# Splitting the state readout of an S5 block into quarters between quarters of a gate unit

## The chip, the cores and the metric

The kernel runs on one NeuronCore of a Trainium2 chip. Its engines are TensorE (PE, matmuls), VectorE (DVE), ScalarE (ACT), GpSimd (POOL) and SyncE (SP); the last two mostly issue transfers here, which all run on the core's 16 DMA engines. The metric is the device time of one execution in microseconds (us), as the median of several runs.

## The reference

One transformer-like block on 256 tokens of width 1024, in float32. The parts around the change:

```python
def s5_readout(h_re, h_im, c_re, c_im):
    y = (jnp.einsum('blgn,ghn->blgh', h_re, c_re) - jnp.einsum('blgn,ghn->blgh', h_im, c_im))
    return y.reshape(y.shape[0], y.shape[1], S5_WIDTH)
...
y_a, y_ac = s5_mixer(u_a, u_ac, ...)          # two scans (forward, backward), readout, then s5_glu
y_b = sgu_mixer(z_b, ...)
...
def s5_glu(y, w, b):
    y = jax.nn.gelu(y)
    return y * jax.nn.sigmoid(y @ w + b)

def merge_branches(y_a, y_b, gate_logits, w_proj_a, w_proj_b, b_gate, w_out):
    g_a, g_b = jnp.split(jax.nn.sigmoid(gate_logits + b_gate), N_BRANCH, axis=-1)
    return (g_a * (y_a @ w_proj_a) + g_b * (y_b @ w_proj_b)) @ w_out
```

Behind it come a modulated norm and a convolutional feed-forward part (`w_up`, a 3 x 3 depthwise convolution, `w_down`). The modulation vectors are `c_silu @ w_ada + b_ada`. `gate_logits` are 2048 columns of `h @ w_in`.

## The kernel before

The program of each engine is written out by hand, in its order; semaphores tie them together. An engine does nothing out of order, so a wait holds up all that stands behind it.

The scan works in chunks of eight tokens. The output of a token is a part from within its chunk (a Toeplitz product, L638) plus what the states carried into the chunk give, the **carry readout** (L651). Both add up in PSUM banks 0 and 1: bank `g2` takes groups of parity `g2`. The readout loops over the two banks, the directions `d` and real and imaginary parts `r`, and 16 groups: 128 matmuls of 64 rows by 32 columns of weights on 128 columns, written as one block of 64 for bank 0 and one of 64 for bank 1. It waits for `s_scan`, VectorE's last carry.

**Gate units** (`gate_unit`, L556) are the eight products that give `gate_logits`, 16 matmuls of 128 x 128 on 256 columns each. Their weights come through a ring of four slots (`ring_w`). Units 1 to 5 run ahead of the Toeplitz product, unit 6 between it and the readout, unit 7 behind the readout. After them PE transposes the eight pieces of the scan's output (L661), does three half projections with y_b (L670), the GLU product (L688), the half projection of m = 3, and then the second halves and the later projections, m = 0 to 7; then the products with w_out (L711, `out_product`).

What the others do there:

- ScalarE copies banks 0 and 1 to SBUF (L921) once `s_y8_ps` is 2, does the sigmoids of gate unit 7 (L880), the gelu (L929), and the sigmoids of the GLU (L933).
- VectorE does `modulation_sums` (L1402): 28 dot products, each on a tile of `mod_w` (512 KB) in one of seven slots. Sums 0 to 11 and L1407 stand ahead of the y rows (L1415, scan output plus skip), sums 12 to 17 behind them, then the four y_a products (L1423), sums 18 and 19, and then the merges of m = 0 to 7 (L1434 to L1437) with one sum, 20 + m, behind each of the first six. L1444 and L1448 prepare the products of L711.
- POOL's queue (q0) loads the tiles of `mod_w`, tile t once sum t - 7 is done. Between tiles 19 and 20 stands the **ga1 store** (L379), 1024 single float32 elements written to a scratch tensor in HBM; ahead of it POOL waits for `s_y8_ps` 2 and `s_ga1`.
- SP's queue (q1) loads ring units: unit u once unit u - 4 has been multiplied. Unit 19 (needed by m = 4 and 5) follows gate unit 7, and after it come a wait for `s_y8_ps` 2 and `out_w[0]`; unit 20 (m = 6 and 7) and `out_w[1]` follow the GLU product.

Of the kernel before, what the change touches and what calls it, by code (L numbers as in the profile page):

```python
# [22 lines left out]
P = 128  # L23
D = 1024
KD = D // P
TOK = 256
# [8 lines left out]
T = 8  # L35
# [9 lines left out]
RING = 4  # L45
# [3 lines left out]
U_ADA1, U_INU, U_V, U_ZU, U_GATE = 0, 2, 4, 6, 8  # L49
GATES = 8  # L50
# [30 lines left out]
def build(nc, x_t, x_tok, ctx_t, pk, s5raw, early_w, ring_w, out_w, up_w, ln, sgu_w, sgu_b, mod_w, c_row, g_row, out):  # L81
    with ExitStack() as ctx:
# [6 lines left out]
        bank = [ctx.enter_context(nc.psum_tensor(f"bank{i}", [P, 512], F32)) for i in range(8)]  # L89
# [6 lines left out]
        ca = ca_region.rearrange("p (d r q e h) -> p d r q e h", d=2, r=2, q=PAIRS, e=T + 1)  # L96
# [24 lines left out]
        h_x = h_all[:, :, TOK:2 * TOK]  # L121
# [7 lines left out]
        ring = ring_region[:, :].rearrange("p (s n) -> p s n", s=RING)  # L129
# [85 lines left out]
        s_unit = sem("unit_multiplied")  # L215
# [25 lines left out]
        s_e_ps, s_e, s_ev, s_scan = sem("e_in_psum"), sem("e_evacuated_by_act"), sem("e_evacuated_by_dve"), sem("carry_ready")  # L241
        s_gate = sem("gate_ready")
        s_mod2, s_scale2 = sem("mod2_ready"), sem("scale2_ready")
        s_y8_ps, s_y8, s_y_tr = sem("y_by_chunk_in_psum"), sem("y_by_chunk_ready"), sem("y_transposed")
# [36 lines left out]
        def ring_ready(pe, u):  # L281

            pe.wait_ge(s_ring[u % RING], 16 * (u // RING + 1))
# [116 lines left out]
        def _(pe):  # L400
# [21 lines left out]
            for k in range(KD):  # L422
                pe.wait_ge(s_sqx[k % 2], k // 2 + 1)
                mx = partial_squares(bank[6], k, TOK)
            mx.then_inc(s_part, 1)
            for k in (1, 2, 0, 3, 5, 6, 4, 7):
                by = next(e for e in range(3) if k in CTX_SQUARES[e])
                pe.wait_ge(s_sqc[by], CTX_SQUARES[by].index(k) + 1)
                mx = partial_squares(bank[7], k, 0)
# [87 lines left out]
            for half in range(2):  # L517
                u = U_V + half
                ring_ready(pe, u)
                for c in range(2):  # L520
                    for kk in range(KD // 2):
                        k = half * (KD // 2) + kk
                        mx = pe.matmul(bank[6 + c][:, :], h_x[:, k, c * P:(c + 1) * P], ring[:, u % RING, kk * 512:(kk + 1) * 512],  # L523
                                       start=(k == 0), stop=(k == KD - 1))
# [8 lines left out]
            for i in range(2):  # L533
                u = U_ZU + i
                ring_ready(pe, u)
                for mm in range(2):
                    for k in range(KD):
                        mx = pe.matmul(bank[2 + i][:, mm * TOK:(mm + 1) * TOK], ring[:, u % RING, (mm * KD + k) * P:(mm * KD + k + 1) * P],
                                       h_x[:, k, :], start=(k == 0), stop=(k == KD - 1))
# [16 lines left out]
            def gate_unit(j):  # L556
                u = U_GATE + j
                ring_ready(pe, u)
                if j >= 2:
                    pe.wait_ge(s_gate, 2 * (j - 1))  # L560
                for mm in range(2):
                    for k in range(KD):
                        mx = pe.matmul(bank[5 - j % 2][:, mm * TOK:(mm + 1) * TOK], ring[:, u % RING, (mm * KD + k) * P:(mm * KD + k + 1) * P],  # L563
                                       h_x[:, k, :], start=(k == 0), stop=(k == KD - 1))
                mx.then_inc(s_unit, 1)
# [15 lines left out]
            for m in range(KS):  # L581
                base = (m % 2) * LAGS * H
                for d, r, e0, j0 in ((1, 0, 1, 0), (1, 1, 1, 0), (0, 0, 0, T - 1), (0, 1, 0, T - 1)):
                    for q in range(4 * m, 4 * m + 4):
                        row = 32 * (q % 4)
                        mx = pe.matmul(bank[6 + m // 2][row:row + 32, base + j0 * H:base + (j0 + T) * H],
                                       b_pad[:, r, d * PAIRS + q].rearrange("p g h -> p (g h)"),
                                       ca[:, d, r, q, e0:e0 + T, :].rearrange("p e h -> p (e h)"),
                                       start=(d == 1 and r == 0), stop=(d == 0 and r == 1), skip_group_check=True)
# [11 lines left out]
            for j in range(4):  # L601
                for c in range(2):
                    for g2 in range(2):
                        mx = pe.matmul(bank[6 + j // 2][g2 * 64:(g2 + 1) * 64, (j % 2) * TOK + c * P:(j % 2) * TOK + (c + 1) * P],
                                       v_tok[:, c, (2 * j + g2) * 64:(2 * j + g2 + 1) * 64], sgu_w_sb[:, j, g2 * P:(g2 + 1) * P],
                                       start=True, stop=True)
# [26 lines left out]
            for g2 in range(2):  # L633
                for j in range(P // H // 2):
                    for m in range(KS):
                        g = m * (P // H) + 2 * j + g2

                        mx = pe.matmul(bank[g2][m * CH:(m + 1) * CH, j * P:(j + 1) * P], u_chunk[:, g, CH:2 * CH], m_toep[:, g, :],  # L638
                                  start=(j == 0), stop=False, skip_group_check=True)
# [1 line left out]

            gate_unit(6)

            pe.wait_ge(s_scan, 1)
            for g2 in range(2):
                half = slice(g2 * N, (g2 + 1) * N)
                for d, r, e0 in ((0, 0, 1), (0, 1, 1), (1, 0, 0), (1, 1, 0)):
                    for j in range(P // H // 2):
                        for m in range(KS):
                            q = m * (P // H // 2) + j  # L650
                            mx = pe.matmul(bank[g2][m * CH:(m + 1) * CH, j * P:(j + 1) * P], carry[half, (r * 2 + d) * PAIRS + q, :],  # L651
                                           ca[half, d, r, q, e0:e0 + T, :].rearrange("p e h -> p (e h)"),
                                           start=False, stop=(d == 1 and r == 1), skip_group_check=True)
                mx.then_inc(s_y8_ps, 1)

            gate_unit(7)


            pe.wait_ge(s_y8, 2)
# [137 lines left out]
        def _(act):  # L797
# [118 lines left out]
            gate_sigmoids(6)  # L916


            act.wait_ge(s_y8_ps, 2)
            for b in range(2):  # L920
                act.activation(y_tok.rearrange("p (t g b h) -> p b g t h", t=T, b=2, h=H)[:, b],  # L921
                               bank[b][:, :].rearrange("p (g t h) -> p g t h", g=4, t=T), ACT.Copy).then_inc(s_y8, 1)

# [825 lines left out]
```

## Time and profile before

| | |
|---|---|
| median of 3 runs | 479.42 us (478.02 to 479.83) |
| span of the profiled execution, first to last instruction | 471.4 us |
| PE busy | 454.4 us, 96% |
| DVE busy | 403.4 us, 86% |
| ACT, POOL busy | 105.2 us, 47.3 us |
| HBM traffic | 206 GB/s over the span |

The profiled execution has no total of its own beside its span; what lies around the span is taken from the median, 8.0 us. Times in the rows are counted from the start of the span. A float32 matmul of the program stands as two records. A bracket at the end of a timeline row says how long the engine stood idle before it and what released it. "issue" means that nothing in the profile explains the idle time.

### The profile page before, as it was taken

The numbers are of one execution on the slowest core, as the hardware profiler recorded it, in microseconds if no ns is written. First come the engines' busy times: TensorE is split into PE (matmuls) and PEld (weight loads), VectorE is DVE, ScalarE is ACT, GpSimd is POOL, SyncE is SP. The second block draws the span as 40 slices with busy tenths as digits, with TensorE's granted clock in tenths as the row PEclk, the third lists the DMA queues.
The fourth block names the chain that finished last, engine by engine and source line by source line (L and its number), as shares of the span: only waits on it lengthen the run. The fifth ranks groups of instructions, "written<-read, shape, count | busy, mean of one in ns | idle before, by whom it ended". The sixth has DMA issues, their size and how long they took to land.

```text
span 471.4 us, 7799 instructions
## 1 busy us (share of the span) xinstructions
PE 454.4 (96%) x2670; PEld 350.5 (74%) x2670; DVE 403.4 (86%) x836; ACT 105.2 (22%) x197; POOL 47.3 (10%) x78
## 2 busy tenths in 40 slices
PE   8899999999999899998999999999999999999994
PEld 5677757888888788883578888887888887444454
DVE  4698999999999857869855999998999999899644
ACT  5432344144113014101151211011011011200002
POOL 2001200004030323200000110110111011000000
PEclk9999999999999979999989999999999999999998
DMA  8993489825999999996985443442443444100002
GB/s 302 421 418 139 163 311 98 332 99 94 115 319 413 417 407 334 240 423 246 426 359 222 179 156 118 173 179 95 172 176 108 161 178 135 43 0 1 0 1 89
DMA packets 22107, 97.41 MB, mean 207 GB/s; under 512 B 6528, under 2 KB 7168, under 8 KB 13376
## 3 DMA queue, kind: packets, MB, share of 16 engines
q1 hardware_dynamic: 15024, 74.70, 44.4%
q0 software_dynamic: 5664, 20.72, 14.9%
q10 hardware_dynamic: 1392, 1.63, 1.0%
q8 instruction: 18, 0.29, 0.3%
q14 instruction: 9, 0.07, 0.1%
HBM read 94.44 MB, written 2.59 MB: 206 GB/s over the span
## 4 chain that ended last, share of the span: by engine, by line
PE 69%; DVE 18%; DMA 8%; issue 2%; ACT 1%; SPq 1%; DVEq 0%; ACTq 0%
PE bank L759 31%; PE bank L770 14%; PE bank L563 11%; DVE s_region L1033 8%; DMA s_region<-early_w 4%; DMA s_region<-mod_w 4%; PE bank L711 4%; PE bank L478 3%; PE bank L651 2%; PE bank L688 1%; DVE s_region L1152 1%; PE bank L670 1%; DVE s_region L1290 1%; PE bank L443 1%; DVE merge_tmp L1033 1%
## 5 line engine op out<-in xcount | busy, mean ns | idle before, releaser
L759 PE MATMUL bank<-h_all,s_region 128*128 128x256 f32 x704 | 153.5, 381 | 0.7 <-ACT ctx_region L982 0.7
L759 PEld LDWEIGHTS bank<-h_all,s_region 128*128 128x128 f32 x704 | 134.5, 191 | 19.5 <-ACT ctx_region L982 1.1
L1561 DVE SCALAR_TENSOR_TENSOR ctx_region<-ctx_region,pk_sb 128x189 f32<-128x189 f32 (+2 forms) x352 | 127.6, 437 | 0.2 <-DVE ctx_region L1561 0.2
L563 PE MATMUL bank<-h_all,ring_region 128*128 128x256 f32 x256 | 58.4, 390 | 0.7 <-DVE s_region L1321 0.7
L563 PEld LDWEIGHTS bank<-h_all,ring_region 128*128 128x128 f32 x256 | 49.9, 196 | 8.7 <-DVE s_region L1321 1.0
L770 PE MATMUL bank<-s_region,ring_region 128*128 128x512 f32 (+1 forms) x132 | 47.6, 521 | 0.0
L770 PEld LDWEIGHTS bank<-s_region,ring_region 128*128 128x128 f32 x132 | 25.1, 190 | 22.6 <-issue 21.5
L982 ACT ACTIVATE ctx_region<-bank 128x512 f32<-128x512 f32 x22 | 13.1, 597 | 127.3 <-PE bank L759 70.6
L1402 DVE SCALAR_TENSOR_TENSOR s_region<-s_region 128x1024 f32<-128x1024 f32 x28 | 33.3, 1223 | 7.8 <-DMA s_region<-mod_w 7.5
L1033 DVE TENSOR_TENSOR s_region<-s_region,power 128x2048 f32<-128x2048 f32 (+1 forms) x16 | 38.1, 2420 | 0.2
L395 POOL TENSOR_TENSOR ring_region<-gates,ctx_region 128x256 f32 x22 | 17.2, 784 | 184.6 <-ACT gates L987 184.6
L1551 DVE TENSOR_SCALAR ctx_region<-ctx_region,pk_sb 128x256 f32<-128x256 f32 x44 | 21.0, 521 | 14.5 <-ACT ctx_region L982 13.2
L478 PE MATMUL bank<-h_all,ring_region 128*128 128x256 f32 x128 | 31.2, 389 | 0.0
L670 PE MATMUL bank<-z_region,ring_region 128*128 128x256 f32 x128 | 28.0, 379 | 0.0
L478 PEld LDWEIGHTS bank<-h_all,ring_region 128*128 128x128 f32 x128 | 23.2, 190 | 5.5 <-issue 2.5
L670 PEld LDWEIGHTS bank<-z_region,ring_region 128*128 128x128 f32 x128 | 24.2, 190 | 3.3
L382 POOL DMA_DIRECT2D s_region<-mod_w x28 | 14.8, 538 | 43.1 <-DVE s_region L1402 43.1
L880 ACT ACTIVATE gates<-bank,pk_sb 128x256 f32<-128x256 f32 x16 | 6.7, 470 | 44.2 <-PE bank L563 44.2
L523 PE MATMUL bank<-ring_region,h_all 128*128 128x512 f32 x32 | 16.4, 593 | 0.0
L1002 ACT ACTIVATE z_region<-s_region 128x512 f32<-128x512 f32 (+1 forms) x5 | 2.7, 541 | 52.8 <-DVE s_region L1614 30.0
L511 PEld LDWEIGHTS bank<-ident,s_region 128*128 128x128 f32 x64 | 7.9, 141 | 8.8 <-issue 7.9
L711 PE MATMUL bank<-s_region,h_all 128*128 128x512 f32 (+1 forms) x40 | 14.2, 507 | 0.0
(236 smaller groups left out, 502.6 us busy)
## 6 DMA issues: line engine op xcount, KB each, us to landing
s_region<-up_w SPq DMA_DIRECT2D x33, 1024.0 KB, 4.8
ring_region<-ring_w SPq DMA_DIRECT2D x22, 1024.0 KB, 10.6
s_region<-mod_w POOLq DMA_DIRECT2D x28, 512.0 KB, 10.3
s_region<-early_w SPq DMA_DIRECT2D x4, 1024.0 KB, 21.7
s_region<-out_w SPq DMA_DIRECT2D x4, 1024.0 KB, 11.9
gates<-early_w SPq DMA_DIRECT2D x2, 1024.0 KB, 10.7
s_region<-k_scratch POOLq DMA_DIRECT2D x8, 256.0 KB, 11.8
x_region<-x_t SPq DMA_DIRECT2D x1, 1024.0 KB, 4.9
```

What stands on the lines that cost most here:

```text
L395: pool.tensor_tensor(ffn_act[:, bass.ds(i * 2 + b, 1), :].rearrange("p a t -> p (a t)"), silu_sb[:, b, :], conv[:, b, TOK:2 * TOK], ALU.mu ...
L478: mx = pe.matmul(bank[m][:, cols], ring[:, U_INU + k // 4, ((k % 4) * KS + m) * P:((k % 4) * KS + m + 1) * P], h_all[:, k, cols], start=(k ...
L523: mx = pe.matmul(bank[6 + c][:, :], h_x[:, k, c * P:(c + 1) * P], ring[:, u % RING, kk * 512:(kk + 1) * 512], start=(k == 0), stop=(k == K ...
L563: mx = pe.matmul(bank[5 - j % 2][:, mm * TOK:(mm + 1) * TOK], ring[:, u % RING, (mm * KD + k) * P:(mm * KD + k + 1) * P], h_x[:, k, :], st ...
L670: mx = pe.matmul(bank[PROJ_BANK[m % 4]][:, (1 - half) * TOK:(2 - half) * TOK], ring[:, u % RING, t * P:(t + 1) * P], src[:, k, :], start=( ...
L711: mx = pe.matmul(bank[OUT_BANK[n]][:, cols], lhs(i), rhs(i)[:, cols], start=(i == 0 and n not in (2, 3)), stop=(i == KD // 2 - 1), skip_gr ...
L759: mx = pe.matmul(bank[s % 3][:, half * TOK:(half + 1) * TOK], up_ring[:, s, (half * KD + k) * P:(half * KD + k + 1) * P], h2[:, k, :], sta ...
L770: mx = pe.matmul(bank[PRODUCT_BANK[n]][:, cols], lhs(i), rhs(i)[:, cols], start=(i == 0), stop=(i == PAIRS_D - 1))
L1033: mark(dve.tensor_tensor(o, a, b, op))
L1402: dve.scalar_tensor_tensor(out=mod_tile[t % MTS], in0=mod_tile[t % MTS], scalar=1.0, in1=c_bc, op0=ALU.mult, op1=ALU.mult, accum_out=mod_s ...
L1551: dve.tensor_scalar(dst[half], src[half], cw[:, tile[half], 4], par("conv_b")[:, tile[half]], ALU.mult, ALU.add).then_inc(s_conv, 1)
L1561: dve.scalar_tensor_tensor(out=o, in0=a, scalar=cw[:, tile[half], (dy + 1) * 3 + dx + 1], in1=o, op0=ALU.mult, op1=ALU.add).then_inc(s_con ...
```

## The change

The readout is cut into four quarters, by bank and direction. Gate unit 7 is cut into quarters of four matmuls, by half of its columns and half of its inner dimension, and one follows each quarter of the readout. The waits of the gate unit stand ahead of its first quarter. `s_y8_ps` is counted up after each bank's second quarter, and ScalarE copies bank 0 when it is 1 and bank 1 when it is 2.

```diff
--- before.py
+++ after.py
@@ -641,19 +641,39 @@
 
             gate_unit(6)
 
-            pe.wait_ge(s_scan, 1)
-            for g2 in range(2):
+            def carried(g2, d):
+
                 half = slice(g2 * N, (g2 + 1) * N)
-                for d, r, e0 in ((0, 0, 1), (0, 1, 1), (1, 0, 0), (1, 1, 0)):
+                for r in range(2):
                     for j in range(P // H // 2):
                         for m in range(KS):
                             q = m * (P // H // 2) + j
                             mx = pe.matmul(bank[g2][m * CH:(m + 1) * CH, j * P:(j + 1) * P], carry[half, (r * 2 + d) * PAIRS + q, :],
-                                           ca[half, d, r, q, e0:e0 + T, :].rearrange("p e h -> p (e h)"),
+                                           ca[half, d, r, q, 1 - d:1 - d + T, :].rearrange("p e h -> p (e h)"),
                                            start=False, stop=(d == 1 and r == 1), skip_group_check=True)
-                mx.then_inc(s_y8_ps, 1)
-
-            gate_unit(7)
+                if d == 1:
+                    mx.then_inc(s_y8_ps, 1)
+
+            def last_gate_part(mm, k0):
+
+                u = U_GATE + GATES - 1
+                for k in range(k0, k0 + KD // 2):
+                    mx = pe.matmul(bank[4][:, mm * TOK:(mm + 1) * TOK], ring[:, u % RING, (mm * KD + k) * P:(mm * KD + k + 1) * P],
+                                   h_x[:, k, :], start=(k == 0), stop=(k == KD - 1))
+                if mm == 1 and k0 > 0:
+                    mx.then_inc(s_unit, 1)
+
+            pe.wait_ge(s_scan, 1)
+            carried(0, 0)
+            ring_ready(pe, U_GATE + GATES - 1)
+            pe.wait_ge(s_gate, 2 * (GATES - 2))
+            last_gate_part(0, 0)
+            carried(0, 1)
+            last_gate_part(0, KD // 2)
+            carried(1, 0)
+            last_gate_part(1, 0)
+            carried(1, 1)
+            last_gate_part(1, KD // 2)
 
 
             pe.wait_ge(s_y8, 2)
@@ -916,8 +936,8 @@
             gate_sigmoids(6)
 
 
-            act.wait_ge(s_y8_ps, 2)
             for b in range(2):
+                act.wait_ge(s_y8_ps, b + 1)
                 act.activation(y_tok.rearrange("p (t g b h) -> p b g t h", t=T, b=2, h=H)[:, b],
                                bank[b][:, :].rearrange("p (g t h) -> p g t h", g=4, t=T), ACT.Copy).then_inc(s_y8, 1)
```

On PE, around the readout (`bank0` and `bank1` take the scan's output, `bank4` gate unit 7; `x_region` holds the carries, `ring_region` the ring; L661 of the changed kernel is the gate part, L651 the readout in both). Before:

```order
L651 MATMUL bank0<-s5_region,x_region 32x128 [waits carry_ready]
L651 MATMUL bank0<-s5_region,x_region 32x128 x63
L651 MATMUL bank1<-s5_region,x_region 32x128 x64
L563 MATMUL bank4<-h_all,ring_region 128x256 [waits gate_ready,ring_loaded3]
L563 MATMUL bank4<-h_all,ring_region 128x256 x15
L661 MATMUL bank0<-ident,ctx_region 128x128 [waits y_by_chunk_ready]
```

The same stretch of the changed kernel:

```order
L651 MATMUL bank0<-s5_region,x_region 32x128 [waits carry_ready]
L651 MATMUL bank0<-s5_region,x_region 32x128 x31
L661 MATMUL bank4<-h_all,ring_region 128x256 [waits gate_ready,ring_loaded3]
L661 MATMUL bank4<-h_all,ring_region 128x256 x3
L651 MATMUL bank0<-s5_region,x_region 32x128 x32
L661 MATMUL bank4<-h_all,ring_region 128x256 x4
L651 MATMUL bank1<-s5_region,x_region 32x128 x32
L661 MATMUL bank4<-h_all,ring_region 128x256 x4
L651 MATMUL bank1<-s5_region,x_region 32x128 x32
L661 MATMUL bank4<-h_all,ring_region 128x256 x4
L681 MATMUL bank0<-ident,ctx_region 128x128 [waits y_by_chunk_ready]
```

The 16 matmuls of the gate unit have moved from behind the readout to between its quarters, and between the last readout matmul and the first transpose there are 4 large matmuls where there were 16.

On ScalarE, the copies of the two banks, before and then after, with the sigmoids of gate unit 7 behind them:

```order
L921 ACTIVATE ctx_region<-bank0 128x4x8x16 [waits y_by_chunk_in_psum]
L921 ACTIVATE ctx_region<-bank1 128x4x8x16
L880 ACTIVATE gates<-bank4,pk_sb 128x256 [waits unit_multiplied]
L880 ACTIVATE gates<-bank4,pk_sb 128x256
L926 ACT_TABLE_LOAD
```

```order
L941 ACTIVATE ctx_region<-bank0 128x4x8x16 [waits y_by_chunk_in_psum]
L941 ACTIVATE ctx_region<-bank1 128x4x8x16 [waits y_by_chunk_in_psum]
L900 ACTIVATE gates<-bank4,pk_sb 128x256 [waits unit_multiplied]
L900 ACTIVATE gates<-bank4,pk_sb 128x256
L946 ACT_TABLE_LOAD
```

The order is the same; the second copy has a wait of its own. The rows of SP, POOL and VectorE have not moved.

## Rows read from the trace of the kernel before

**Rows 1.** The page: span, and busy time of PE with its share and instructions.

```profile
span 471.4 us, 7799 instructions
PE 454.4 (96%) x2670; PEld 350.5 (74%) x2670; DVE 403.4 (86%) x836; ACT 105.2 (22%) x197; POOL 47.3 (10%) x78
```

**Rows 2.** The chain of work that ended last: start us, us, what.

```profile
191.22 18.27 DMA s_region<-mod_w
...
216.27 17.42 PE bank L711 x40
```

**Rows 3.** Timeline of PE, 148 to 211: start us, us, what, count.

```profile
148.76 7.17 PE L563 MATMUL bank<-h_all,ring_region 128*128 128x256 f32 x32
155.87 3.96 PE L651 MATMUL bank<-s_region,x_region 64*32 64x128 f32 x151
161.97 4.23 PE L651 MATMUL bank<-s_region,x_region 64*32 64x128 f32 x105 [2.14 <-issue]
166.12 9.37 PE L563 MATMUL bank<-h_all,ring_region 128*128 128x256 f32 x32
...
181.38 7.07 PE L688 MATMUL bank<-u_x,ring_region 128*128 128x256 f32 x32
...
188.29 22.61 PE L670 MATMUL bank<-z_region,ring_region 128*128 128x256 f32 x104
```

**Rows 4.** Windows: us, busy of PE PEld DVE ACT POOL, PE clock, DMA share, GB/s.

```profile
155.90:159.80 3.90, 3.90 (x152) 3.66 (x152) 3.90 (x9) 0.84 (x2) 1.59 (x3) 1.00 1.01 415
159.80:162.00 2.20, 0.06 (x7) 0.03 (x5) 2.20 (x4) 0.00 (x0) 1.05 (x2) 1.00 0.98 402
163.80:170.60 6.80, 6.80 (x57) 5.52 (x49) 4.40 (x9) 1.09 (x2) 1.82 (x4) 0.50 1.02 405
```

**Rows 5.** DMA view of 159 to 162: queue, packets, MB, share of 16 engines.

```profile
q8 instruction: 1, 0.02, 2.3%
```

**Rows 6.** Timeline of ACT, the copies and the gelu.

```profile
166.23 1.09 ACT L921 ACTIVATE ctx_region<-bank 128x512 f32<-128x512 f32 x2 [9.42 <-PE bank L651]
...
178.24 2.11 ACT L929 ACTIVATE u_x<-ctx_region 128x1024 f32<-128x1024 f32 x1 [0.35 <-DVE ctx_region L1415]
```

**Rows 7.** Timeline of SP's issues, 170 to 195.

```profile
175.90 0.43 SPq L329 DMA_DIRECT2D s_region<-out_w  x1
188.49 0.33 SPq L321 DMA_DIRECT2D ring_region<-ring_w  x1
```

**Rows 8.** Timeline of DVE, 172 to 211.

```profile
172.66 0.17 DVE L1407 TENSOR_TENSOR mod<-mod_sum,pk_sb 128x8 f32<-128x8 f32 x1
176.05 2.15 DVE L1415 SCALAR_TENSOR_TENSOR ctx_region<-u_x,pk_sb,bank 128x128 f32<-128x128 f32 x8 [3.22 <-PE bank L661]
...
189.00 0.79 DVE L1423 TENSOR_TENSOR z_region<-u_x,ctx_region 128x256 f32<-128x256 f32 x2 [2.66 <-ACT ctx_region L933]
...
194.29 1.23 DVE L1402 SCALAR_TENSOR_TENSOR s_region<-s_region 128x1024 f32<-128x1024 f32 x1 [1.06 <-DMA s_region<-mod_w]
...
209.59 1.23 DVE L1402 SCALAR_TENSOR_TENSOR s_region<-s_region 128x1024 f32<-128x1024 f32 x1 [1.40 <-DMA s_region<-mod_w]
```

**Rows 9.** DMA view of 172 to 176, the only data queue in it.

```profile
q0 software_dynamic: 448, 1.62, 101.8%
```

**Rows 10.** DMA view of 180 to 185.

```profile
q1 hardware_dynamic: 207, 1.47, 71.2%
q0 software_dynamic: 164, 0.54, 29.4%
```

**Rows 11.** Timeline of POOL, 176 to 182.

```profile
180.16 0.92 POOL L379 DMA_DIRECT2D ga_scratch<-mod  x1
```

**Rows 12.** DMA: 178 to 196, issue and us to landing; 190 to 195, queues.

```profile
ga_scratch<-mod POOLq DMA_DIRECT2D x1, 4.0 KB, 13.5
...
q0 software_dynamic: 161, 0.59, 93.1%
```

**Rows 13.** DMA issues at 188.5: SP's ring unit 20, us to landing.

```profile
ring_region<-ring_w SPq DMA_DIRECT2D x1, 1024.0 KB, 14.9
```

## The prediction

> **What bounds the kernel now.** I read the page first: span 471.4 us, PE busy for 96% of it [rows 1]. That invites the thought that each microsecond saved on PE is a microsecond of time. The chain of waits says otherwise for the place of the change. After the readout it runs for a while over PE, but from 191.22 to 209.49 it is one transfer, a tile of mod_w (18.27 us), and only at 216.27 does it come back to PE's product loop L711 [rows 2]. So two questions have to be kept apart: what the change does to PE around 156 to 176, and whether that reaches 216.27.
>
> The timeline of PE shows three losses around the readout L651 [rows 3]. It is recorded as 256 matmuls (two records to each of the 128 written in the loop). The first 151 take 3.96 us, 26.2 ns each; then PE stands for 2.14 us with no releaser ("issue"); the other 105 take 4.23 us, 40 ns each. The gate unit behind them, 32 records, takes 9.37 us, where the same 32 took 7.17 us ahead of the readout. The windows explain the last two: the granted clock is 0.50 from 163.8 to 170.6, that is 1.2 GHz in place of 2.4; before the stall, with small matmuls alone, it is 1.00, and in the stall PE is busy for 0.06 us of 2.20 at a DMA share of 0.98 [rows 4]. In that stretch the instruction queue q8 has one packet of 0.02 MB [rows 5]. I take the stall for a late instruction packet: two short instructions for every 26 ns use them up faster than anywhere else, and the DMA engines are full.
>
> **The change, part by part.** *Order on PE.* The same matmuls run, in eight pieces. A quarter of the readout is 64 records, 1.68 us; a quarter of the gate unit is 8 records, 1.79 us [rows 3]. Two gate parts (3.6 us) now lie inside the first 151 small records, more than the 2.14 us by which the packet came late, so the stall should go; bounds 0 and 2.14 us of it left. With no stall and every 1.7 us a stretch of full-size matmuls, I expect the clock to stay at 2.4 GHz. Sum: stall 2.14, the slow 105 records 4.23 - 2.75 = 1.48, the gate unit 9.37 - 7.17 = 2.20: 5.8 us. PE comes to the transposes at 169.7, not 175.5. Changing between small and large matmuls six times more shows no price: the records before and after L651 overlap.
>
> The Trainium skill, Runtime: NRT & Kernel Launch, section Instruction fetch mechanics, speaks against the first term: PE's instruction memory holds 2048 instructions and dispatch is said to be slower than the fetch. By it the 2.14 us would be something else and stay, and the sum here would be 3.7 us or, if the clock follows the stall, 0. The trace has the packet in the stall's own window, so I go by the row.
>
> *ScalarE's copies.* Two copies take 1.09 us, 0.55 each [rows 6]. Bank 0 is copied under the third quarter. Bank 1 is complete at 167.9, its copy ends about 168.6, and the last gate part runs until 169.7, so it costs nothing; the spare is 1.1 us where it was 8. Without that cover the cost is 0.6.
>
> *What waits behind.* s_y8_ps reaches 2 at 167.9, against 166.2 before: SP's and POOL's waits on it have later conditions anyway (gate unit 7 for SP, sum 12 for POOL), nothing lost. SP issues ring unit 19 and out_w[0] when the gate unit is through, before at 175.5, with the unit done, and 175.90 [rows 7], then near 169.8: that is 2 MB more in the DMA queues 5.8 us earlier.
>
> **Where the gain goes.** First VectorE. It works in order and still has modulation sums 0 to 11 to do, each paced by a landing tile; they end with L1407 at 172.66, long after nothing of PE's is wanted [rows 8]. The y rows L1415 began at 176.05, now at 172.85: gain 3.2. ScalarE's gelu ended at 180.35 [rows 6], 4.3 us behind L1415's start, so now at 177.2; the GLU matmuls, which started at 181.38 because PE was the late one [rows 3], start at 177.3, gain 4.1; PE waits 1.6 us for them.
>
> Second the tiles 12 to 17. From 172 to 176 POOL's queue q0 had the DMA engines alone, 1.62 MB in 4 us, 101.8% [rows 9]; with both queues at work q1 gets 1.47 MB in 5 us and q0 0.54 [rows 10]. The 2 MB that SP now issues at 170 begin to move about 172.3 (from 172 to 176 q1 does not appear though its unit was issued at 175.5, so they are some 2.5 us on the way) and need some 7.5 us; meanwhile a tile (0.52 MB) takes 3.7 us, not 1.3. Tile 17 lands near 183.9, VectorE is through with its sum at 185.1 and with the four y_a products at 186.7. They ended at 189.79 before [rows 8]. PE, through with projection(3,0) at 186.1, starts the second halves at 186.8, before at 188.29 + 8 records = 190.1 [rows 3]. Gain left: 3.3 us.
>
> Third, and for good, the ga1 store. POOL issues it at 180.16 and it lands 13.5 us later, at 193.7 [rows 11, 12]. It is 4 KB in single elements. While it is worked on, the engines move little: from 190 to 195 only q0 appears, 0.59 MB, a quarter of the usual rate, and q1 moves nothing although SP issued a unit at 188.49 [rows 7, 12]; that unit took 14.9 us to land [rows 13]. Tile 20 is queued behind the store: VectorE waited for it until 194.29 [rows 8]. When can the store begin? In 172 to 176 and in 180 to 185 the shares of the queues add up to 100% [rows 9, 10]: the DMA engines are full until about 185, with tiles up to 19, unit 19 and out_w[0]. The change reorders these bytes and removes none. So the store begins at about 185.5 in either kernel, lands near 193.7, and tile 20 lands at 194.2. From 195 on the two queues are full again, and tiles 21 to 25 arrive at the pace of q0's third. The wait for tile 25 ends at 209.5 [rows 2, 8]; behind it VectorE does L1444, the last merge and L1448, for which PE's L711 waits until 216.27 [rows 2]. PE needs ring unit 20 for m = 6: it lands at 203.4, PE now comes at 201 and waits 2.4 us. It ends its projections at 210.5 and the first product at 214.1, before 216.27 still. The whole lead of 3.3 us is eaten between 194 and 209.5. Sum against the span: 5.8 on PE, 0 at the end; 471.4 stays 471.4. The span lies 8.0 us under the median of 479.42 (no total of the profiled execution itself is given), and I carry that.
>
> **Rivals.**
> *SP's unit and out_w[1] fill the dead time of the store.* They are now issued near 184.3, ahead of the store's work and not in its midst. If their 2 MB move between 186 and 195, q1 is through 7 us earlier (0.29 MB per us [rows 10]), and tiles 24 and 25 come at 1.3 us, not 3.7: 4.8 us earlier, of which PE's lead lets 3.3 through. Time 476.1 to 477.5. Against it: q1 moved nothing from 190 to 195 with a unit waiting. The Trainium skill, DMA: Bandwidth & Descriptors, section Queues, rings and completion order, says that an engine takes turns between its queues packet by packet, which would let q1 in; the row of 190 to 195 disagrees. Chance 0.28, nine tenths of it beyond 0.5%.
> *The same 2 MB push the tiles back.* They take turns with the store and q0's 118 GB/s, and do not fill idle time: tile 20 lands up to 5 us later (2 MB at 0.41 MB per us), tiles 21 to 25 follow with less q1 beside them. It decides from the moment that tile 25 lands after 209.6; each microsecond more is one of time. Price 1 to 3.5 us, time 480.4 to 482.9. Chance 0.18, some five sixths of it beyond 0.5%, with up to 2.2 us for a clock that falls while PE waits.
> *Nothing changes on PE* (the stall stays, or the clock falls in spite of the gate parts). The end does not move either: 479.4. Chance 0.08.
> *The forecast*: 5.8 us won on PE, lost in the wait for the tiles. Chance 0.46; own range 478.3 to 480.4.
>
> **How the numbers follow.** I predict 479.3. Half a per cent, 2.4 us, is about what a measurement of this kernel can tell from no change. Faster by more: 0.9 x 0.28 = 0.25. Slower: five sixths of 0.18 = 0.15. Same: 0.60, the forecast, the unchanged PE and the near ends of the two rivals. The range goes to the ends of both rivals without their last tenth: 476.2 to 481.9.
>
> **What would show it.** Right: no "issue" gap in the readout, granted clock 1.00 from 156 to 176, transposes at about 169.7, GLU at 177.3; VectorE's waits for mod_w longer in total than before; tile 20 at 194 and tile 25 at 209 to 210; L711's wait ending near 216. Wrong: the stall back in the second half of the readout; a store that lands before 192; ring unit 20 landing before 200, with tile 25 before 207 (faster), or tile 20 after 197 (slower).

## The result

Over 21 runs of each the changed kernel takes 480.80 us, the kernel before 475.93 us (the first three runs of it, 479.42 in the median, had been on the high side). The ratio is 1.0086, with a 95% interval of 1.0062 to 1.0110: slower, by about 4 us. The time lies inside the range of the prediction, 476.2 to 481.9, but the forecast was no change.

The page of the changed kernel: its span and busy times. PE has the same 2670 matmuls; its busy time is up by 4 us, and the share stays at 96%.

```profile
span 479.5 us, 7799 instructions
PE 458.6 (96%) x2670; PEld 349.9 (73%) x2670; DVE 403.9 (84%) x836; ACT 105.3 (22%) x197; POOL 47.7 (10%) x78
```

This span must not be set against 471.4 [rows 1] as it stands. In this execution the last k_scratch transfer, long ahead of the change, let POOL issue `c_row` and the first tiles at 141.34; in the profile of before it was 136.94. No row above the readout explains that by the change, and in the experiments below it lies between 136.9 and 141.0 with the old order on PE and between 136.5 and 141.3 with the new one. So I count from that issue to the end where two profiles are compared: 334.5 us before, 338.2 after, a difference of 3.7 us where the ratio gives 4.1. This is POOL's timeline, first before and then after:

```profile
136.94 0.57 POOL L374 DMA_DIRECT2D s_region<-c_row  x1 [19.62 <-DMA s_region<-k_scratch]
```

```profile
141.34 0.61 POOL L374 DMA_DIRECT2D s_region<-c_row  x1 [22.29 <-DMA s_region<-k_scratch]
```

The timeline of PE in the changed kernel, against [rows 3]:

```profile
157.01 1.95 PE L651 MATMUL bank<-s_region,x_region 64*32 64x128 f32 x64
158.89 1.99 PE L661 MATMUL bank<-h_all,ring_region 128*128 128x256 f32 x8
160.82 1.95 PE L651 MATMUL bank<-s_region,x_region 64*32 64x128 f32 x64
...
172.14 1.04 PE L681 MATMUL bank<-ident,ctx_region 128*128 128x128 f32 x8
173.01 5.34 PE L690 MATMUL bank<-z_region,ring_region 128*128 128x256 f32 x24
181.48 8.83 PE L708 MATMUL bank<-u_x,ring_region 128*128 128x256 f32 x32 [3.12 <-ACT u_x L949]
190.14 22.76 PE L690 MATMUL bank<-z_region,ring_region 128*128 128x256 f32 x104
212.74 2.74 PE L731 MATMUL bank<-s_region,h_all 128*128 128x512 f32 x6
217.43 1.10 PE L731 MATMUL bank<-s_region,h_all 128*128 128x512 f32 x2 [1.96 <-DVE h_all L1457]
221.61 6.23 PE L731 MATMUL bank<-x_region,gates 128*128 128x512 f32 x8 [3.08 <-DVE gates L1468]
```

The reader is to see two things. The local gain is there: from the first readout matmul to the first transpose 15.1 us, where it was 19.5 [rows 3], with no "issue" gap. And the gain comes back as waits: 3.1 us ahead of the GLU product (L708), 2.0 us inside the first product with w_out and 3.1 us behind it, ahead of the second. Behind the last of them the eight records that took 3.67 us before take 6.23. The windows say why: us, busy of PE PEld DVE ACT POOL, granted clock, DMA share, GB/s.

```profile
157.00:172.10 15.10, 15.10 (x289) 12.62 (x289) 9.22 (x17) 2.03 (x4) 3.70 (x7) 1.00 1.02 412
...
217.40:219.90 2.50, 1.10 (x2) 0.30 (x2) 2.50 (x3) 0.60 (x1) 0.00 (x0) 1.00 1.00 411
219.90:226.70 6.80, 5.09 (x6) 2.19 (x7) 6.66 (x12) 0.00 (x0) 0.00 (x0) 0.50 0.27 103
226.70:231.00 4.30, 4.30 (x11) 1.90 (x10) 3.78 (x4) 0.60 (x1) 0.00 (x0) 0.99 0.99 345
```

The clock stays at 2.4 GHz through all the quarters, against 1.2 GHz from 163.8 to 170.6 before [rows 4]. Instead it falls behind two of the waits. The first time is in the GLU product, with a granted clock of 0.70 from 184 to 187; the product takes 8.83 us where it took 7.07 [rows 3], and with it goes a part of PE's lead. The second time is at 219.9, until 226.7, and that is on the chain: the chain of waits of the changed kernel (start us, us, what) goes through a tile, VectorE and this product, which opens the 19.98 us of L731 that were 17.42 [rows 2].

```profile
193.08 21.75 DMA s_region<-mod_w
...
221.61 19.98 PE bank L731 x40
```

### The profile page after: what moved, and what is told of

Read it like the earlier page. It is cut to its first block, busy times and chain, and to the rows that moved or that the text cites. A ratio compares the mean times of both kernels' runs of the same rounds, so it can differ in the third digit from the quotient of the medians.

```text
span 479.5 us, 7799 instructions
## 1 busy us (share of the span) xinstructions
PE 458.6 (96%) x2670; PEld 349.9 (73%) x2670; DVE 403.9 (84%) x836; ACT 105.3 (22%) x197; POOL 47.7 (10%) x78
## 4 chain that ended last, share of the span: by engine, by line
PE 57%; DMA 19%; DVE 17%; ACT 2%; issue 2%; POOL 1%; SPq 0%; DVEq 0%; ACTq 0%; POOLq 0%
PE bank L779 31%; PE bank L790 14%; DMA s_region<-mod_w 11%; DVE s_region L1053 8%; DMA s_region<-k_scratch 5%; PE bank L731 4%; PE bank L478 4%; DMA gates<-early_w 3%; PE bank L708 2%; PE bank L443 1%; DVE s_region L1172 1%; DVE s_region L1310 1%; DVE s_region L1422 1%; POOL s_region L370 1%; DMA k_scratch<-s_region 1%
## 5 line engine op out<-in xcount | busy, mean ns | idle before, releaser
L563 PE MATMUL bank<-h_all,ring_region 128*128 128x256 f32 x224 | 49.0, 380 | 0.2 <-DVE s_region L1341 0.2
L790 PE MATMUL bank<-s_region,ring_region 128*128 128x512 f32 (+1 forms) x132 | 47.6, 521 | 0.0
L563 PEld LDWEIGHTS bank<-h_all,ring_region 128*128 128x128 f32 x224 | 42.4, 190 | 6.3 <-DVE s_region L1341 0.4
L478 PE MATMUL bank<-h_all,ring_region 128*128 128x256 f32 x128 | 31.9, 395 | 0.0
L478 PEld LDWEIGHTS bank<-h_all,ring_region 128*128 128x128 f32 x128 | 23.7, 194 | 6.0 <-issue 2.9
L731 PE MATMUL bank<-s_region,h_all 128*128 128x512 f32 (+1 forms) x40 | 14.5, 509 | 2.0 <-DVE h_all L1457 2.0
L538 PE MATMUL bank<-h_all,ring_region 128*128 128x256 f32 x64 | 14.0, 379 | 0.0
```

The costliest lines, as they stand in the source:

```text
L478: mx = pe.matmul(bank[m][:, cols], ring[:, U_INU + k // 4, ((k % 4) * KS + m) * P:((k % 4) * KS + m + 1) * P], h_all[:, k, cols], start=(k ...
L731: mx = pe.matmul(bank[OUT_BANK[n]][:, cols], lhs(i), rhs(i)[:, cols], start=(i == 0 and n not in (2, 3)), stop=(i == KD // 2 - 1), skip_gr ...
L790: mx = pe.matmul(bank[PRODUCT_BANK[n]][:, cols], lhs(i), rhs(i)[:, cols], start=(i == 0), stop=(i == PAIRS_D - 1))
```

## The experiments

Of the twelve runs eleven were timed in turn with the kernel before, and their ratio is to that kernel. In each profile I read from VectorE's timeline where the sums of tiles 20 and 25 start, from POOL's when `c_row` is issued, and from PE's how long the second product with w_out takes. The table has them all, also the two of the result; the sums are counted from `c_row`'s issue. The kernel with the filler had one execution of 968.52 us among its 12, which is not in its ratio.

| kernel | ratio (95% interval) | c_row | sum 20 | sum 25 | second product | c_row to end |
|---|---|---|---|---|---|---|
| before | 1 | 136.9 | 57.3 | 72.7 | 3.67 | 334.5 |
| changed | 1.0086 (1.0062 to 1.0110) | 141.3 | 56.8 | 73.6 | 6.23 | 338.2 |
| changed again | 1.0077 (1.0037 to 1.0117) | 138.0 | 58.0 | 74.8 | 6.11 | 339.2 |
| changed, SP later | 1.0111 (1.0051 to 1.0171) | 136.5 | 56.6 | 75.4 | 6.46 | 340.4 |
| changed, copies together | 1.0101 (1.0057 to 1.0145) | 139.1 | 58.1 | 74.1 | 6.35 | 338.9 |
| changed, filler | 1.0010 (0.9959 to 1.0062) | 140.4 | 57.5 | 74.6 | 3.67 | 336.5 |
| before, filler | 1.0008 (0.9976 to 1.0039) | 138.8 | 57.9 | 72.6 | 3.60 | 335.8 |
| changed, hold | 0.9933 (0.9893 to 0.9973) | 138.8 | 55.5 | 69.9 | 3.67 | 330.5 |
| before, hold | 0.9959 (0.9931 to 0.9987) | 137.9 | 55.6 | 70.9 | 3.67 | 332.9 |
| changed, filler and hold | 0.9986 (0.9951 to 1.0021) | 139.4 | 55.5 | 70.2 | 3.60 | 335.1 |
| before, row store | 0.9921 (0.9885 to 0.9958) | 141.0 | 54.7 | 66.7 | 3.60 | 329.5 |
| changed, row store | 0.9878 (0.9821 to 0.9935) | 138.1 | 52.9 | 67.3 | 3.67 | 328.0 |
| changed, row store and hold | 0.9892 (0.9841 to 0.9943) | 138.5 | 53.1 | 65.1 | 3.60 | 327.8 |
| before, 80 instructions more at the start | one run | 139.4 | 57.7 | 72.4 | 3.67 | 333.0 |

One thing must be known for the last column. In all of these profiles PE changes over to the product with `w_up` some 23 us behind the end of the second product. In eight of the 14 the granted clock falls there for some 3.5 us (0.79 on average from 240 to 248 in the kernel before), and then 251.5 to 251.8 us lie between the end of the second product and the end of the kernel; in the other six it stays at 1.00, and there are 250.2 to 250.3. The kernel before has this fall and so have all changed ones with the old store and no hold, but the kernel before with filler and the one with 80 instructions more have not. No run here shows what decides it. So some 1.3 us of a difference between two rows of this column can be that alone: the 334.5 and 338.2 both contain it, of the pair 330.5 (without) and 332.9 (with) it is more than half.

**The changed kernel again.** No edit.

> The changed kernel once more, for a second profile and a second ratio. Open from the first profile: it differs from that of before already ahead of the change (the last k_scratch tile landed at 140.8 us, before at 136.9). Theory A (the loss is the change's own: PE waits longer for VectorE and for the tiles, 3.1 us ahead of the GLU product and 3.1 us ahead of the second product with w_out, and the granted clock falls to 0.50 behind both waits, which costs 2.5 us on the path behind the second): ratio 1.006 to 1.011 again, both waits and the low clock there whether k_scratch is early or late. Theory B (the difference of the two profiles is chance in k_scratch, and the change costs what the pushed-back tiles cost): ratio again above 1, but with k_scratch at 137 the clock stays 1.00 behind the second wait and tile 25 lands at 210 or later.

The ratio is 1.0077. With `c_row` at 138.0, near the 136.9 of before, both effects are there: tile 25 is 2.1 us later than in the kernel before, and the clock falls. The low stretch is even longer, 10.2 us, as the windows show (columns as above):

```profile
210.00:214.20 4.20, 1.61 (x4) 0.38 (x2) 3.73 (x8) 0.00 (x0) 0.00 (x0) 0.99 1.01 412
214.20:224.40 10.20, 6.97 (x8) 2.69 (x9) 9.99 (x16) 0.60 (x1) 0.00 (x0) 0.50 0.35 143
```

PE's timeline of this run has the wait ahead of it:

```profile
208.87 2.74 PE L731 MATMUL bank<-s_region,h_all 128*128 128x512 f32 x6
215.30 2.05 PE L731 MATMUL bank<-s_region,h_all 128*128 128x512 f32 x2 [3.69 <-DVE h_all L1457]
219.47 6.11 PE L731 MATMUL bank<-x_region,gates 128*128 128x512 f32 x8 [2.13 <-DVE gates L1468]
```

PE is through with its projections 2 us earlier than in the kernel before [rows 3] and then, inside the first product, stands for 3.69 us.

Theory B in the form that I gave it, chance in k_scratch and a clock that stays, is refuted; its tile 25 at 210 or later is seen (212.8).

**SP's unit 19 and out_w[0] issued later.**

```diff
                 sp.wait_ge(s_unit, u - RING + 1)
+                if u == U_PROJ + 2:
+                    sp.wait_ge(s_y, KS)
```

> The changed kernel, but SP issues ring unit 19 and out_w[0] only after four y rows, about as late as before the change. Theory A (clock behind PE's waits): ratio stays within 0.002 of the changed kernel's, since PE waits as long. Theory B (the 2 MB issued early push back tiles 12 to 19, the store and tile 25): tiles 12 to 17 come at 1.3 us again, the wait for y_a shrinks, and the ratio goes back to 1.000 to 1.003.

Ratio 1.0111: not the way back that theory B forecast. The sums of tiles 12 to 17 do end sooner, and the y_a products too. SP's next unit is asked for at 184.3, that is 47.8 us behind `c_row`, as early as in the changed kernel (49.0 and 47.6), and tile 25 comes at 75.4, the latest of all. What SP issues early at 170 is not the cost.

**Filler for PE's waits**, in the changed kernel and, as a control, in the kernel before. The nine matmuls compute nothing that is used.

```diff
+                    if n == 1 and i == KD // 2 - 1:
+                        busy(3)
...
+            busy(6)
             pe.wait_ge(s_to, 1)
             pe.wait_ge(s_so, 1)
```

> The changed kernel with 9 idle-time matmuls (ones by ones into free bank 3, 0.44 us each): three ahead of the last part of the first product with w_out, six ahead of the second product, where PE waited 2.0 and 3.1 us in the first profile. Theory A (clock): granted clock 1.00 behind the second wait, the second product's 8 records take 3.7 us and not 6.2, and the ratio falls by 0.004 to 0.005 against the changed kernel's. Theory B (tiles): nothing gained, up to 0.5 us lost where the filler ends late.

> The same 9 idle-time matmuls in the kernel before, as a control. PE waited 1.9 us there and the clock stayed at 1.00 in the first profile, so 4.0 us of filler end up to 2 us late. Both theories: ratio 1.000 to 1.004; below 1 only if in most executions of the kernel before the clock falls there too, which would shrink what theory A can explain.

PE's timeline of the changed kernel with filler:

```profile
217.46 1.10 PE L737 MATMUL bank<-s_region,h_all 128*128 128x512 f32 x2 [2.22 <-DVE h_all L1464]
221.64 3.67 PE L737 MATMUL bank<-x_region,gates 128*128 128x512 f32 x8 [0.49 <-DVE gates L1475]
```

The product takes 3.67 us again, and the ratio goes from 1.008 to 1.001. The interval is wide (0.996 to 1.006); the medians of all its runs, 478.43 against 476.39 us, give 1.004, so the size rests on the row more than on the ratio. That the clock is what changed is also seen in the timed runs, each of which has a mean granted clock: its median is 0.982 over the 33 runs of the changed kernel and 0.992 over the 12 with filler. Theory A is borne out, for up to its 2.5 us. The same filler leaves the kernel before at 1.0008. That is no clean control: its profile has the second product start 82.0 us behind `c_row`, 2.6 us later than without filler (79.3), since 4 us of filler do not fit into a wait of 1.9, so a loss and a gain may cancel there. Tile 25 stays late in the changed kernel, at 74.6, so theory A is not all.

**Unit 20 and out_w[1] held back** until the ga1 store has landed.

```diff
                 sp.wait_ge(s_unit, u - RING + 1)
+                if u == U_PROJ + 3:
+                    sp.wait_ge(s_ga1_out, 16)
```

> The changed kernel, but SP issues ring unit 20 and out_w[1] only when the ga1 store has landed. So far the sum of tile 20 starts 56.6 to 58.0 us behind the issue of c_row in every profile, while that of tile 25 starts 72.6 us behind it in the two profiles without the change and 73.6 to 75.4 in the four with it. Theory B' (SP's unit, now asked for 4 us earlier, gets its two thirds of the DMA engines as soon as the store is through, and tiles 21 to 25 are pushed back): tile 25 goes back to 72.4 to 73.0 us, the clock stays low behind PE's waits, ratio 1.004 to 1.007. Theory A (clock alone): tile 25 as in the changed kernel, ratio unchanged at 1.008.

> Control for the hold: the kernel before, with ring unit 20 and out_w[1] issued only when the ga1 store has landed. There SP asks at 188.5, 5 us ahead of the landing, and its bytes move from 195 anyway. Theory B' (the changed kernel is slower because SP's earlier unit gets ahead of tiles 20 to 25): nothing to win here, tile 25 at 72 to 73 us behind c_row, ratio 0.998 to 1.003, and the hold's gain of 0.015 belongs to the changed order alone. Rival (the hold is a gain by itself, and the quarters bring nothing): tile 25 at 70 us, ratio 0.993 to 0.996.

The hold takes 0.0144 off the ratio of the changed kernel and 0.004 off the kernel before, so 0.010 of it belongs to the changed order, as much as the whole loss. Tile 25 comes at 69.9, 4.9 us earlier than in the changed kernel's second profile. That is VectorE's timeline, sums that waited for their tile; first the changed kernel, second profile:

```profile
195.97 1.23 DVE L1422 SCALAR_TENSOR_TENSOR s_region<-s_region 128x1024 f32<-128x1024 f32 x1 [4.73 <-DMA s_region<-mod_w]
199.18 1.23 DVE L1422 SCALAR_TENSOR_TENSOR s_region<-s_region 128x1024 f32<-128x1024 f32 x1 [0.85 <-DMA s_region<-mod_w]
202.90 1.23 DVE L1422 SCALAR_TENSOR_TENSOR s_region<-s_region 128x1024 f32<-128x1024 f32 x1 [1.36 <-DMA s_region<-mod_w]
206.66 1.22 DVE L1422 SCALAR_TENSOR_TENSOR s_region<-s_region 128x1024 f32<-128x1024 f32 x1 [1.40 <-DMA s_region<-mod_w]
210.40 1.22 DVE L1422 SCALAR_TENSOR_TENSOR s_region<-s_region 128x1024 f32<-128x1024 f32 x1 [1.38 <-DMA s_region<-mod_w]
```

and with the hold:

```profile
194.33 1.23 DVE L1424 SCALAR_TENSOR_TENSOR s_region<-s_region 128x1024 f32<-128x1024 f32 x1 [2.53 <-DMA s_region<-mod_w]
197.16 1.22 DVE L1424 SCALAR_TENSOR_TENSOR s_region<-s_region 128x1024 f32<-128x1024 f32 x1 [0.47 <-DMA s_region<-mod_w]
...
208.70 1.22 DVE L1424 SCALAR_TENSOR_TENSOR s_region<-s_region 128x1024 f32<-128x1024 f32 x1 [1.38 <-DMA s_region<-mod_w]
```

The first five rows are tiles 20 to 24, from tile 21 on 3.7 us apart: each has to share the DMA engines from the start. With the hold the sums of 22 and 23 start without a wait (60.7 and 63.1), 2.4 us apart, which is VectorE's own pace there, and the row at 208.70 is tile 25 itself. The DMA view of 195 to 200 has the same in bytes, first the changed kernel's second profile, then the hold:

```profile
q1 hardware_dynamic: 167, 1.25, 60.5%
q0 software_dynamic: 188, 0.68, 37.6%
```

```profile
q0 software_dynamic: 360, 1.29, 69.3%
q1 hardware_dynamic: 60, 0.49, 23.2%
```

So SP's unit is what pushes tiles 21 to 25 back, as theory B' says. The numbers that I gave for it were too small: tile 25 comes at 69.9 and not at 72.4, and the clock that I expected to stay low does not. PE's longest wait in this stretch is now the 1.8 us for unit 20, it waits 0.5 us ahead of the second product, and the mean granted clock of the profile is 0.999, where it was 0.982. The gain of the hold is thus tiles and clock together, and this run does not part them. My control was wrong by the hold's own gain of 0.004: tile 25 comes 1.8 us earlier even in the kernel before. Tile 20 comes earlier too in all three profiles with the hold, at 55.5 or 55.6 against 56.6 to 58.1, so a unit of SP's that waits behind the store costs something in either order. Between the two orders with the hold, 0.9933 and 0.9959, the intervals overlap: a gain of the quarters themselves is not shown.

**Filler and hold together.**

> The hold and the 9 idle-time matmuls together. If clock and pushed-back tiles are the whole loss: tile 25 at 72.4 to 73.0 us behind c_row, the second product's 8 records 3.7 us, ratio 0.998 to 1.002, as with the filler in the kernel before (1.0008). If something else of the change costs time, the ratio stays above 1.003.

The ratio, 0.9986, is as expected, but tile 25 comes at 70.2 and not at 72.4, and the hold alone does better (0.9933). With the hold there are hardly any waits left to fill, so the nine matmuls (4 us) now cost most of what they take: the second product starts 79.7 us behind `c_row`, with the hold alone 76.5.

**The ga1 store in rows.** PE transposes the eight columns, ScalarE copies the 8 x 128 block, POOL stores eight rows of 512 bytes.

```diff
-                    pool.dma_start(ga1_dram[:].rearrange("a (k p) -> p (a k)", p=P), mod2[:, 0:KD], allow_slow_non_contiguous=True).then_inc(s_ga1_out, 16)
+                    pool.dma_start(ga1_dram[:].rearrange("a (k p) -> (a k) p", p=P), ga1_rows[0:KD, :]).then_inc(s_ga1_out, 16)
...
+            pe.wait_ge(s_ga1, 1)
+            pe.transpose(bank[3][0:KD, 0:P], mod2[:, 0:KD], ident[:, :]).then_inc(s_ga1_ps, 1)
             ring_ready(pe, U_GLU)
...
+            act.wait_ge(s_ga1_ps, 1)
+            act.activation(ga1_rows[0:KD, :], bank[3][0:KD, 0:P], ACT.Copy).then_inc(s_ga1_rows, 1)
```

> The kernel before, with the 1024 single elements of the ga1 store replaced by eight rows of 512 bytes: PE transposes the 8 columns ahead of the GLU product, ScalarE copies them behind its gelu, POOL stores them. The forecast's pin (the DMA engines move little for 8 us while the store is worked on, and tiles 20 to 25 stand behind it): tile 20 lands 6 to 8 us earlier, the wait ahead of the second product goes, and PE's own work bounds this stretch: ratio 0.988 to 0.996. Rival (the dead time is not the store's): tile 20 as before, ratio 0.999 to 1.003.

> The changed kernel with the same row store. If the store is the pin, PE's lead is no longer eaten: the changed kernel comes 2 to 4 us ahead of the kernel before with the row store (ratio 0.980 to 0.990), with no low clock behind the second product's wait. If the tiles' bytes alone are the pin, the two row-store kernels are equal or the changed one is slower again.

The kernel before with rows has 0.9921, no wait for any tile from 20 on, and q0 moves 1.79 MB from 190 to 195 where it was 0.59 [rows 12]:

```profile
q0 software_dynamic: 496, 1.79, 89.8%
q1 hardware_dynamic: 36, 0.29, 14.3%
```

The wait ahead of the second product is gone, as expected; the sum of tile 25 starts 6 us earlier. The changed order on top gives 0.9878: the medians are 471.39 and 470.21 us, the ratios 0.004 apart with intervals that overlap. The 2 to 4 us that I expected between the two are not confirmed; the profiles, both without the fall of the clock behind the product, show 1.5 us.

**Row store and hold together**, SP's unit 20 waiting for sum 19 (`s_mt_used` 20).

> The version meant to beat both kernels: the changed order, the ga1 store in eight rows of 512 bytes, and ring unit 20 and out_w[1] held until sum 19 is done. Theory B' and the store as a pin: tiles 20 to 25 come ahead of SP's unit, tile 25 at 66 to 68 us behind c_row, PE's own work bounds the stretch, ratio 0.982 to 0.989. If unit 20 comes too late for m = 6, PE waits for it and the ratio is 0.988 to 0.993, no better than the row store alone.

Ratio 0.9892, no better than the row store alone (0.9878), although tile 25 comes at 65.1: PE does not wait from the first product with w_out to the end of the second, so tiles no longer bound that stretch. Both versions are faster than the kernel before and the changed kernel; against the kernel before with rows (0.9921) neither is told apart.

**The other part of the change undone**: the changed order on PE, ScalarE waits for both banks.

```diff
+            act.wait_ge(s_y8_ps, 2)
             for b in range(2):
-                act.wait_ge(s_y8_ps, b + 1)
```

> The changed order on PE without the other part of the change: ScalarE waits for both banks and copies them together (1.09 us) under the last gate part (1.8 us). All theories: the y rows of VectorE start as in the changed kernel, ratio 1.006 to 1.012, within 0.003 of the changed kernel's. If the transposes start later by up to 0.2 us, nobody waits for them, since VectorE comes later.

Ratio 1.0101, inside the changed kernel's interval. No effect of copying one by one is seen; the loss belongs to the order on PE.

**The stall**, in the kernel before with 20 matmuls of one column (80 instructions, 40 records) at the program's start.

> The kernel before with 20 matmuls of one column at the program's start, 80 instructions more on PE, 1 to 2 us. If the stall in the readout is the arrival of an instruction block, it moves with the count of instructions: 40 records earlier, behind about 111 of the 256 and not behind 151, and the stall in L552 moves from behind 188 records to behind about 148. If it is tied to the place in the program or to a bank (the change from bank 0 to bank 1 is at 128), it stays at 151.

```profile
100.25 5.82 PE L555 MATMUL bank<-ctx_region,s_region 128*64 128x64 f32 x192
...
159.07 6.36 PE L654 MATMUL bank<-s_region,x_region 64*32 64x128 f32 x239
167.49 0.70 PE L654 MATMUL bank<-s_region,x_region 64*32 64x128 f32 x17 [2.06 <-issue]
```

The stall moved, but not to 111: it stands behind record 239, and the one in L552 is gone. 239 is 111 + 128, so the next block boundary if a block is 256 instructions (a record has its weight load). In this one profile it has moved with the count of instructions and has not stayed at its place in the program. That it is the arrival of a block remains an inference from that. Why the boundary at 111 was passed in time is open; it is reached 1.1 us earlier in the dense stretch than the old one at 151.

## Why the prediction was wrong

**The local part** was right in kind and too large. The "issue" gap is gone and the clock is 1.00 throughout. The sum was 5.8 us; measured are 4.3 (19.46 against 15.13 us from the first readout matmul to the first transpose). The term that I set at nothing is the changing between small and large matmuls: a quarter of the readout takes 1.88 us instead of 1.68, a gate part 1.93 instead of 1.79, 1.3 us over all eight; that the changing causes it is my reading, no run varies it alone. On the rule of the Trainium skill, Runtime: NRT & Kernel Launch, section Instruction fetch mechanics, that fetching is hidden behind dispatch: if the stall is a late fetch, the traces do not agree, since the stall of 2.1 to 2.3 us is in all five profiles of the unchanged order and in none of the nine with the quarters, and moved with the number of instructions. That section also gives blocks of 256 instructions, and with those the distance of 128 records agrees.

**VectorE and the tiles up to 19** went as forecast. Tile 20's sum starts 56.6 to 58.1 us behind `c_row` in all profiles with the old store and no hold, with the change and without: the bytes ahead of the store are the same. The lead of PE when it starts the second halves was forecast at 3.3 us; against `c_row` the second profile of the changed kernel has 187.88 - 138.01 = 49.9, before it was 190.1 - 136.94 = 53.1: 3.2 us. In the first profile, with its slower GLU product, it is 2.6 us.

**The step that failed** is the one behind it: "From 195 on the two queues are full again, and tiles 21 to 25 arrive at the pace of q0's third", the same in both kernels. In the kernel before SP's unit 20 is asked for 51.6 us behind `c_row` (50.6 to 52.4 in the three profiles of that order), and the sums of tiles 20 to 22 start at 57.3, 59.8 and 62.2. In the changed kernel and its versions with the old store and no hold it is asked for at 47.6 to 50.2, and its bytes move sooner once the store is through: from 195 to 200 q1 has 1.25 MB and q0 0.68 in the second profile of the changed kernel, before 1.01 and 0.89. Tile 25 comes 1 to 3 us later: 73.6 to 75.4 against 72.4 to 72.7. The time of the request does not fix the size alone: requests at 50.2 (copies together) and 50.6 (80 instructions more) have tile 25 at 74.1 and 72.4. This is my second rival, with a price inside its range of 1 to 3.5 us, though its mechanism was a bit different: tile 20 comes no later than in the kernel before. The first rival, filling of the dead time, did not come: from 190 to 195 q1 moved 0.01 MB in the second profile of the changed kernel. The Trainium skill, DMA: Bandwidth & Descriptors, section Queues, rings and completion order, would have its packets take turns there; in none of these rows do they. Behind the store they do: from 200 to 205 the two queues have 191 and 192 packets.

**The second step that failed**: "PE ... waits 2.4 us" for unit 20, and ends its first product at 214.1, so that only 2.1 us of waiting were left ahead of 216.27. The prediction moved the unit's request to 184.3 and left its landing at 203.4. Unit 20, asked for earlier, also landed earlier (201.0 in the second profile), so PE did not wait there and kept its whole lead up to the first product. There it waited 3.7 and 2.1 us (2.0 and 3.1 in the first profile) with 1 to 2 us of work between, and the granted clock fell, where single waits there of 1.9 us (before) and 2.6 us (80 instructions more) left it at 2.4 GHz. I had put the price of such a fall at up to 2.2 us and inside a rival; it is 2.4 to 2.8 us (3.67 against 6.11 to 6.46), it stands on the chain, and it came in all four changed kernels without filler or hold. The sum goes up: 1.6 us for tile 25 (the mean of 73.6, 74.8 and 74.1 less that of 72.7, 72.6 and 72.4) and 2.5 us for the clock make 4.1 us, 0.9%, against a measured 0.8 to 0.9%.

That the sum meets the result so well is in part luck. Both terms come from single profiles, and the profile of the kernel before is one of its better executions: its mean granted clock is 0.985, while over the 75 timed runs of that kernel that have one it is 0.979 in the median, no higher than the changed kernel's 0.982. So in many runs the kernel before has a low clock in more places than its profile shows. Where these are, and how much of the 2.5 us is left as a difference of the averages, stays open, and so does the share of the fall behind the product, which all changed kernels with the old store and no hold show and of the three such profiles of the old order only one.

**The range** contains 480.80 by luck too. The base of the prediction, 479.42, was the median of three runs; over 21 runs it is 475.93. With the same steps from there the range would end at 478.4. The 8.0 us between span and time were no fixed cost either: in the profiled run of the changed kernel they are 1.8 us (481.33 against 479.5), and the rest was a span of a fast execution set against a median of slower ones.

## What to carry to other kernels

A lead that an engine wins ahead of a bound resource does not just vanish. It makes that engine's next requests earlier, and these can overtake the transfers on the critical path in the shared DMA engines; and it turns into idle time right ahead of critical work, where the clock may be lost. Ask of each gain that is not on the chain: which transfer does it trigger sooner, and what is behind that transfer in the queue? Here one wait on SP turned 0.8% slower into 0.7% faster than the kernel before, of which 0.4% was to be had without the quarters. And count profiles from the last event that they do not share: the two first profiles differed by 4.4 us before the change even began.

## What the runs showed of the hardware

- A store of 4 KB as 1024 single elements held both queues down for some 8 us (q0 at 118 GB/s, q1 at nothing) [rows 12]. Writing it as eight rows of 512 bytes, with the transpose and the copy that this needs, takes 0.8% off the kernel's time (ratio 0.9921).
- With both queues busy, SP's queue takes about two thirds of the bytes and POOL's one third (1.43 and 0.70 MB from 200 to 205 in the second profile of the changed kernel; 1.47 and 0.54 in [rows 10]). A tile of 0.5 MB then takes 3.7 us, where the rate of [rows 9] gives 1.3.
- The last k_scratch transfer lets `c_row` go up to 4.8 us apart from one profile to another. Whether that makes the spread of 472 to 483 us of the kernel before is not shown; what the timed runs do show beside it is the clock: the 32 of 75 runs with a mean granted clock of 0.978 or less have a median of 477.8 us, the 14 with 0.985 or more 473.7.
- PE's stall in the dense small matmuls of the readout costs 2.1 to 2.3 us in five profiles. With 40 records more ahead of it, it moved from record 151 to 239, which is 128 records, or 256 instructions, behind the place where the shift alone would have put it.
